# Modulation rows of the first mixer: accumulated on VectorE instead of TensorE, and their units set among the row units

## The reference

```python
mod = (c_act @ ada_w[l] + ada_b[l])[:, None, :]
sh_m, sc_m, gt_m, sh_f, sc_f, gt_f = jnp.split(mod, 6, axis=-1)
h = rms_norm(x, norm_mix[l]) * (1 + sc_m) + sh_m
y = hybrid_mixer(h, ...)      # gated delta rule (4 heads) and stick-breaking attention (8 heads)
x = x + gt_m * y
h = rms_norm(x, norm_ffn[l]) * (1 + sc_f) + sh_f
```

## Time and profile before

| | us |
|---|---|
| median of 3 runs | 2863.24 |
| lowest, highest | 2859.11, 2866.93 |
| the profiled execution's own time | 2861.78 |
| its span, first to last instruction | 2860.0 |
| TensorE busy (share of the span) | 2762.7 (97%) |
| VectorE busy | 2208.3 (77%) |
| ScalarE busy | 1601.4 (56%) |

### The profile page before, as it was taken

How to read it: one execution, slowest core, us unless ns; L and a number is a source line. 1 busy time by engine, 2 the same in 40 slices (tenths; PEclk the granted TensorE clock), 3 DMA queues, 4 the chain that set the end, 5 groups by cost and what they waited for, 6 DMA issues and landing times.

```text
span 2860.0 us, 45138 instructions
## 1 busy us (share of the span) xinstructions
PE 2762.7 (97%) x16972; PEld 2428.3 (85%) x16972; DVE 2208.3 (77%) x3851; ACT 1601.4 (56%) x2771; POOL 87.0 (3%) x150
## 2 busy tenths in 40 slices
PE   8898999999999999999999999999999999999998
PEld 5676887977888879999998888888899999988886
DVE  4666888886665668999887878865789988778877
ACT  3433554344554644678894554545457789754553
POOL 1000111010002000000000000020000000000000
PEclk9999999999999999999999999999999999999999
DMA  8433777764556235666668777752466665687775
GB/s 294 144 115 128 263 256 250 242 243 155 185 190 231 89 120 182 207 211 202 196 194 266 242 241 242 234 195 68 148 195 213 209 198 193 213 263 242 242 241 164
DMA packets 211289, 579.69 MB, mean 203 GB/s; under 512 B 24097, under 2 KB 87873, under 8 KB 210049
## 3 DMA queue, kind: packets, MB, share of 16 engines
q1 hardware_dynamic: 161568, 491.00, 52.9%
q0 software_dynamic: 13792, 53.28, 5.5%
q10 hardware_dynamic: 35712, 32.52, 3.3%
HBM read 541.05 MB, written 35.65 MB: 202 GB/s over the span
## 4 chain that ended last, share of the span: by engine, by line
PE 83%; DVE 11%; ACT 4%; issue 1%; DMA 0%; ACTq 0%; DVEq 0%; POOLq 0%
PE psum L758 83%; DVE gmem L2155 3%; DVE wr L2155 2%; DVE gmem L2158 2%; ACT gmem L1544 2%; DVE xmem L2158 1%; ACT crf L1544 1%; DVE xr L2155 1%; ACT wr L1544 0%; DVE xmem L2155 0%; DVE small L2934 0%; PE psum L839 0%; DVE gmem L3048 0%; ACT xmem L1544 0%; DMA raw<-in_ada_w 0%
## 5 line engine op out<-in xcount | busy, mean ns | idle before, releaser
L2155 DVE TENSOR_TENSOR wr<-raw,wr 128x1024 fp32r<-128x1024 f32 (+1 forms) x814 | 995.6, 1224 | 415.5 <-ACT wr L1544 411.1
L758 PE MATMUL psum<-xr,wr 128*128 128x256 f32 (+1 forms) x9760 | 1291.7, 292 | 13.9 <-DVE xr L2155 9.3
L758 PEld LDWEIGHTS psum<-xr,wr 128*128 128x128 f32 x9760 | 1236.2, 192 | 57.9 <-DVE xr L2155 14.7
L1544 ACT ACTIVATE wr<-raw 128x1024 fp32r<-128x1024 f32 x808 | 848.0, 1050 | 279.8 <-PE psum L758 258.4
L758 PE MATMUL psum<-wr,cr 128*128 128x512 f32 x3072 | 697.4, 389 | 5.0 <-DVE cr L2155 5.0
L758 PEld LDWEIGHTS psum<-wr,cr 128*128 128x128 f32 x3072 | 576.4, 188 | 125.7 <-ACT cr L1544 3.3
L1544 ACT ACTIVATE cr<-xmem 128x256 fp32r<-128x256 f32 x256 | 107.2, 419 | 337.9 <-PE psum L758 335.8
L1544 ACT ACTIVATE gmem<-psum 128x512 f32<-128x512 f32 (+2 forms) x303 | 169.2, 570 | 215.4 <-PE psum L758 190.1
L758 PE MATMUL psum<-wr,xr 128*128 128x512 f32 (+1 forms) x960 | 237.8, 401 | 8.2 <-DVE gmem L2155 3.7
L758 PEld LDWEIGHTS psum<-wr,xr 128*128 128x128 f32 x960 | 177.1, 194 | 52.5 <-issue 6.5
L2158 DVE SCALAR_TENSOR_TENSOR oh_r<-cst,keep,keep_r 128x256 fp32r<-128x256 f32 x512 | 213.3, 479 | 0.0
(11 more groups left out here) (173 smaller groups left out, 1522.1 us busy)
## 6 DMA issues: line engine op xcount, KB each, us to landing
raw<-in_uv SPq DMA_DIRECT2D x512, 512.0 KB, 4.9
raw<-in_ffn_in SPq DMA_DIRECT2D x88, 512.0 KB, 3.7
gs<-xmem ACTq DMA_DIRECT2D x248, 128.0 KB, 3.7
xmem<-gs SPq DMA_DIRECT2D x248, 128.0 KB, 4.4
gmem<-in_ada_w POOLq DMA_DIRECT2D x56, 512.0 KB, 4.8
raw<-in_ffn_out SPq DMA_DIRECT2D x44, 512.0 KB, 4.2
raw<-in_ada_w SPq DMA_DIRECT2D x40, 512.0 KB, 4.1
raw<-in_ret_a SPq DMA_DIRECT2D x32, 512.0 KB, 4.3
```

The lines of the kernel that those rows point to most:

```text
L758: ins = pe.matmul(o, a, b, start=first and i == 0, stop=final and i == len(pairs) - 1, skip_group_check=skip)
L1544: return act.activation(o, a, func, **k)
L2155: return dve.tensor_tensor(o, a, b, op)
```

## The change

Rows 4, 5, 6 and 8 of the modulation become added rows too, so that all 24 units after the first sixteen are used by VectorE. Their accumulators lie in the buffer `crf` (two of 512 words), rows 4 and 5 first and then 6 and 8; a wait makes the first operation of row 6 (and of 8) come behind the closing product of row 4 (of 5). The block of rows 4 and 5 between the gate's row units and the stick-breaking part's row units is gone: each of its eight units stands behind one of the first eight row units. The steps of the strands between are 5 behind each of the first eight row units and 4 behind each of the last four, instead of 3 everywhere. Four more `add_up` steps come in: rows 4 and 5 behind the last row unit, row 6 behind the tenth unit of `THIRD`, row 8 in front of row 9.

```diff
-    ADDED = (7, 9)
+    ADDED = (4, 5, 6, 7, 8, 9)
...
-    add_plain(SECOND)
-    units += [(dr["hyb_a"][c][i], UNIT) for c in range(1, 4) for i in range(4)]
+    for n in range(12):
+        units.append((dr["hyb_a"][1 + n // 4][n % 4], UNIT))
+        add_plain(SECOND[n:n + 1])
     add_plain(THIRD)
...
-    ada_acc = {m: keepm[:, 512 * i:512 * i + 512] for i, m in enumerate(ADDED)}
+    ada_acc = {m: v[:, 512 * i:512 * i + 512] for v, ms in ((crf, (4, 5)), (crf, (6, 8)), (keepm, (7, 9)))
+               for i, m in enumerate(ms)}
...
         bg.add(s["gdn"]())
-        for i, (m, q) in enumerate(SECOND):
-            if i > 1:
-                bg.run(3)
-            s["modulate"](m, q)
         stick = s["stick"]()
         for c in range(3):
             for i in range(4):
                 s["stick_rows"](c, i)
-                bg.run(3)
+                if c < 2:
+                    s["modulate"](*SECOND[4 * c + i])
+                bg.run(4 if c == 2 else 5)
             if c == 0:
                 s["stick_q"]()
             if c == 1:
                 bg.add(stick)
+        s["add_up"](4)
+        s["add_up"](5)
         for i, (m, q) in enumerate(THIRD):
             s["modulate"](m, q)
             if i % 2:
                 bg.run(6)
+            if i == 9:
+                s["add_up"](6)
             if i == 11:
-                s["add_up"](ADDED[0])
+                s["add_up"](7)
         bg.until_done(stick)
         s["hybrid_turn"](1)
-        s["add_up"](ADDED[1])
+        s["add_up"](8)
+        s["add_up"](9)
...
                 acc = ada_acc[m]
+                if m in (6, 8) and q == 0:
+                    dve.wait_ge(*X.pe["added", 4 if m == 6 else 5])
                 for k in range(2):
...
-                if m == 4:
-                    dve.wait_ge(mod_in, 48)
...
         def add_up(m):
             d = mod_dst(m)
+            if m == 4:
+                dve.wait_ge(mod_in, 48)
             dve.wait_ge(*X.pe["added", m])
```

## The result

| | before | after |
|---|---|---|
| median, us (4 runs each, same chip) | 2861.68 | 2883.64 |
| lowest, highest | 2859.11, 2866.93 | 2881.24, 2890.01 |
| profiled execution: own time, span | 2861.78, 2860.0 | 2881.8, 2879.8 |
| mean granted clock of TensorE | 0.990 | 0.979 |
| VectorE busy, us | 2208.3 | 2230.8 |

The ratio is 1.0076, 95% interval 1.0061 to 1.0090: 22 us slower. Forecast were 2867.0 and a range of 2855 to 2876, with 0.22 for slower.

What follows compares the result with a forecast made beforehand. TensorE was taken to bound the mixer in its long runs only. A lead of 9 us is spent to 0, then a 7 us lag less credits of 1.4 and 1.6 gives +4: 2863.2 + 4 = 2867, range 2855 to 2876.

Steps and rivals of the forecast that it cites:

- Up to 134.7 us: First mixer until the first level's products start: four row units done instead of one, a lead of 9 us.
- 134.7 to 193 us: Chain levels to the second product of scores: TensorE keeps the pace, accumulation hidden, lead 7 to 8 us.
- The new wait: Closing of rows 4 and 5 near 188: VectorE waits 2 to 5 us for TensorE, lead falls to 4 us.
- To 225.1 us: From 188.4 to the last mask: VectorE has 33 us of work plus 4 idle, so the lead falls to 0.
- 225.1 to 247 us: Closings of rows 6 to 9 up to the first output unit, which starts near 254, not 247.00: lag 7 us.
- The clock: Three new TensorE gaps near 113, 163 and 200 lower the clock: 0 to 4 us, in the range only.
- The rival named for the clock: Low clock behind all three gaps and as many more in the scores: +11 us, 2874; chance 0.06.
- VectorE is the bound: From 193 to 247 VectorE has about 49 of 54 us of work, without closing waits: +12 us, 2875; chance 0.16.

Runs made afterwards that it cites:

- def67_ph: after_ph with only VectorE's additions of rows 6 and 7 (and 8 and 9) put later, in front of the first turn of the results; 1.0027.
- def45_ph: after_ph with only VectorE's additions of rows 4 and 5 put later, behind the eighth of the last sixteen units; 1.0075.
- thin8: The kernel before with all eight units of rows 6 and 8 cut on TensorE to 8 of 512 columns, VectorE unchanged; 1.0012.
- after_ph: The changed kernel with strand step counts 6, 5, 3 instead of 5, 4; 1.0097.
- warm45: rows45 with three constant products on TensorE in the gap ahead of the product with the values; 1.0039.
- late_ph: The changed kernel with counts 6, 5, 3, a separate buffer for rows 6 and 8, and later VectorE additions of the closed rows; 1.0026.
- rows45: The change's new order with only rows 4 and 5 newly on VectorE, rows 6 and 8 left on TensorE; 1.0085 against the kernel before.
- cut81: The kernel before with one unit, the second of row 8, cut on TensorE to 8 of 512 columns; 1.0008.
- warm: The changed kernel with 25 constant products on TensorE in six gaps; 1.0056 against the kernel before.
- fill8: The changed kernel with two constant products on TensorE at each of the eight units of rows 6 and 8; 1.0109 against the kernel before.

## Why the prediction was wrong

**"Up to 134.7 us", lead 9: right.** Four row units are done when the first level's products start (133.25 of the timeline, 37.3 us from the gate's silu, 36.5 before). Eight are done 60.2 us from the silu; "near 156" on the timeline of before is 57.8, so 2.4 us of the lead were gone by then.

**"134.7 to 193 us", a lead of 7 to 8: failed.** It was 1.2 us at the second product of scores. Two terms were too small. The level took longer than the 11.6 us laid out, 12.2 us from 148.84 to 161.01: the pair set to end near 159.5, 61.3 us from the gate's silu, ended at 65.0. And the wait ahead of the stick-breaking transposes was 6.57 us, not "some 4". My count took TensorE and VectorE for a level as two sums and the larger as its length; in the trace they also wait for each other within a level (VectorE busy 31.22 of 39.00 us from 131 to 170, TensorE 28.64). With that nearly the whole credit of the sum was gone before the stage in which I spent it.

**"The new wait": right in kind and size, wrong in weight.** It was 2.94 us, up to 193.43 (2 to 5 forecast). def67_ph, with 9.75 us there, shows that even a longer wait costs little, and late additions of rows 4 and 5 (def45_ph) gained nothing clear of noise.

**"To 225.1 us", from lead 4 to 0: failed in size.** The product with the values stands 9.8 us later than before. VectorE was to be free for the two additions at 188.4 of the timeline of before; it began them at 193.43, which is 195.6 there, so some 7 of the 9.8 us came in from the steps before. From there the stage took 39.1 us, not 37: the work was sized right (31.86 us of VectorE for 33), the idle time not (7.6 us for 4). VectorE is busy 31.86 of 39.50 us, 81%, not over 90%: it isn't the bound. TensorE's order has holes of 6.61 and 4.46 us there, and the clock is 0.74. The step held that the units in this stretch lay in a shadow; thin8 bears this out for TensorE's side. It did not see that taking them from there opens gaps at whose end the next product runs at half speed.

**"225.1 to 247 us", lag 7: the largest miss.** The lag grew by 13.6 us, not by 7. I had VectorE wait for row 6's closing until about 231.4, behind a run of 6.74 us; it waited until 242.54 (244.7 there), behind a product at a lower clock that itself began late. The runs on the closings (after_ph, def67_ph) show how much this step can decide: 0.4 to 0.7% for the place of the additions of rows 6 and 7, with the counts 6, 5, 3. Two of my terms, the wait and the clock, were treated as separate and small; here each makes the other longer. Of the step's two credits, 1.4 us for strand steps done earlier fits what comes back behind the first output unit (the spans from the silu on differ by 22.0 us, the lag there is 23.4), but no run tells whose it is; the other, 1.6 us for overlapping starts, wasn't measured.

**"The clock", in the range and not in the sum: failed.** I priced three gaps at 1.2 us each. In the two stages behind 193 the granted clock is 0.74 over 39.5 us and 0.73 over 35.6, which is 10.3 + 9.6 = 19.9 us of full clock not granted, against none before. Not all of it fell on work in the path: warm45 got 4.4 us back at one product. The Trainium skill ("TensorE: Matmul & The Clock Gate", "HAM oscillation — how this bites in real kernels") has the array fall back to half its clock when bursts of matmuls are broken by waits. The traces agree in kind (after_ph: 0.50 behind a gap of 5.59 us); that shorter gaps of 1.2 to 2.6 us stand ahead of low clock too is what these rows show, and the case on the page is one of longer waits. The prediction gave the clock a smaller price than it had here. The rival named for the clock had the mechanism, with a time of 2874 that was still 10 us short of 2883.64.

**What had no step.** The order alone costs 0.54%, and two strand steps take 0.4% of that away. I followed which units move, and took the strands' places at the start of the last sixteen units as given. That it is the step in the strand and not the number of steps as such was argued from the kernels' schedule, and shown only for two sets of counts. Why the change itself is not helped by it is answered only in part: with the counts 6, 5, 3 the closing of row 6 meets the last turn of the scores, and with the counts 5, 4 it follows the product with the values. An order with the old counts and the later additions of rows 6 and 7 alone wasn't tried.

The rival *VectorE is the bound* (2875) came nearest in time, for a reason that the runs don't bear out: late_ph and def67_ph have all of VectorE's new work and lie at 1.0026 and 1.0027. The condition that it named, a level of over 12 us, was just met (12.2).

## What to carry to other kernels

Work taken from an engine is gained only where that engine is the chain; where it filled a wait for another engine, taking it away opens the wait and can cost the clock behind it (thin8: 11 us of work less, nothing gained). When one engine must wait for a reduction that another one closes, price the wait by what is queued behind it, and put the reading of the result as late as its user allows: here the place of two additions of 0.69 us decided 0.4 to 0.7% (def67_ph against after_ph, by the traces and by the ratios). And before an exchange of work between engines is judged, run the new order by itself: here it carried most of the loss, and two steps of a woven strand decided it.

## What the runs showed of the hardware that was not expected

The clock can stay low under full load. The product with the values is 48 matmuls of 64 columns: 5.47 us at full clock (warm45), and 8.14, 9.90, 10.30 and 10.50 us behind gaps of 1.21, 2.60, 1.38 and 5.59 us (the change, rows45, thin8, after_ph), with TensorE busy in all of every 4 us and 0.50 granted (thin8, 228 to 236 us). The length of the gap just ahead does not order these: 1.38 us went with 10.30 and, in cut81, with 8.41; 2.60 with 9.90. Nor does one thinly filled stretch ahead of the product decide it. In thin8 TensorE was busy 1.76 of 4.00 us from 216; the kernel before has nearly the same at the same distance, and keeps its full clock:

```profile
212.00:216.00 4.00, 1.78 (x15) 1.45 (x13) 4.00 (x7) 0.84 (x1) 0.00 (x0) 1.00 0.44 139
224.00:228.00 4.00, 3.89 (x34) 3.69 (x33) 0.76 (x2) 1.41 (x3) 0.00 (x0) 1.00 0.69 232
```

And def67_ph stands still for 4.38 us up to 226.72, falls to 0.50, and is back at full clock in the product, which lies in its run of 6.80 us:

```profile
226.00:230.00 4.00, 3.28 (x11) 2.92 (x12) 3.58 (x6) 0.00 (x0) 0.00 (x0) 0.50 0.75 226
...
234.00:238.00 4.00, 4.00 (x38) 4.00 (x37) 2.73 (x4) 0.60 (x1) 0.00 (x0) 1.00 0.51 145
```

The fall can come inside unbroken work: in rows45 the granted clock is 1.00 from 228 to 230, where the product starts (229.58), and 0.50 from 232. What decides it, these runs leave open.

The Trainium skill ("TensorE: Matmul & The Clock Gate", "What's actually happening") has the array return to full clock once it has been busy for a while. def67_ph agrees (0.50 at 226, 1.00 at 234, with TensorE busy nearly all the time); thin8 doesn't: some 12 us of unbroken work, 226 to 238, passed at 0.50.

Three constant products in a gap went with full speed in the next product (warm45). Two of them didn't in `warm` (8.02 us behind a gap of 2.07), and two in place of each removed unit didn't either (fill8: 10.48 us behind a gap of 2.18).
